# Query weight parts and query tile 1 pulled into the gated part, and a new order at the end of the attention, in a two-layer hybrid encoder step

## What is computed

```
h = rms_norm(x, w_norm1);  proj = h @ w_in          # columns a, gc, gb | q | k, v, u | vg
y_conv = gb * conv3(gc * a)                         # 256 wide
q, k   = partial_rope(q), partial_rope(k)
y_attn = sink_softmax(q @ k.T / 8, band mask) @ v   # 8 heads, 2 kv heads, 512 wide
u  = gelu(u);  vg = layer_norm(gelu(vg), ln_g, ln_b)
y_gmlp = u * (W_s vg + b_s)                         # per chunk of 128 rows, 4 groups, 256 wide
mix = concat(rms_norm(y_conv), rms_norm(y_attn), rms_norm(y_gmlp))   # each with its part of w_group_norm
x = x + mix @ w_out
x = x + relu(rms_norm(x, w_norm2) @ w_ff1)**2 @ w_ff2
```

## Time and profile before

| | us |
|---|---|
| median of 3 runs | 2365.97 |
| lowest, highest | 2364.42, 2366.91 |
| the profiled execution: its own time | 2366.66 |
| the profiled execution: span, first to last instruction | 2364.6 |
| TensorE busy in it | 2303.7 (97%) |
| VectorE, ScalarE, GpSimd busy | 1275.5, 817.8, 125.6 |
| mean granted TensorE clock | 0.991 of full |

### The profile page before, as it was taken

The page is one execution under the profiler, slowest core; times in us unless marked ns, Lnnn a source line. Parts: engine busy times, 40 slices in busy tenths (PEclk is TensorE's granted clock), DMA queues, the critical chain, the costliest instruction groups (busy, mean ns, idle before and its releaser), DMA issues. The chain is left out here.

```text
span 2364.6 us, 32179 instructions
## 1 busy us (share of the span) xinstructions
PE 2303.7 (97%) x12710; PEld 2054.7 (87%) x12710; DVE 1275.5 (54%) x2205; ACT 817.8 (35%) x1697; POOL 125.6 (5%) x223
## 2 busy tenths in 40 slices
PE   7998999999999999999999999999999999999997
PEld 6987878999999988888898877779999999888885
DVE  5226865434344385765752477663334344766766
ACT  4123422444444432122231234234444444222222
POOL 4010100000000000000130100010000000000001
PEclk9999999999999999999999999999999999999999
DMA  6011001346555786656230110114545549766562
GB/s 175 32 33 44 19 29 43 111 174 219 201 185 210 282 318 233 242 194 241 98 70 28 33 45 19 44 37 148 209 176 216 201 170 357 267 233 252 184 232 115
DMA packets 190374, 361.67 MB, mean 153 GB/s; under 512 B 13308, under 2 KB 96800, under 8 KB 190224
## 3 DMA queue, kind: packets, MB, share of 16 engines
q1 hardware_dynamic: 186368, 352.33, 41.1%
q0 software_dynamic: 2704, 3.10, 0.6%
q10 hardware_dynamic: 1152, 4.19, 0.5%
HBM read 228.01 MB, written 131.37 MB: 152 GB/s over the span
## 5 line engine op out<-in xcount | busy, mean ns | idle before, releaser
L1555 PE MATMUL ps<-hT_hi,w_hi 128*128 128x384 f32 x1824 | 614.7, 337 | 2.7 <-DVE x L1208 2.7
L1556 PE MATMUL ps<-hT_lo,w_hi 128*128 128x384 f32 x1824 | 612.9, 336 | 0.0
L1557 PE MATMUL ps<-hT_hi,w_lo 128*128 128x384 f32 x1824 | 612.9, 336 | 0.0
L1556 PE MATMUL ps<-w_lo,ring 128*128 128x512 f32 x896 | 354.7, 396 | 0.0
L1555 PE MATMUL ps<-w_hi,ring 128*128 128x512 f32 x896 | 352.2, 393 | 0.0
L1557 PE MATMUL ps<-w_hi,ring 128*128 128x512 f32 x896 | 352.0, 393 | 0.0
L1555 PEld LDWEIGHTS ps<-hT_hi,w_hi 128*128 128x128 f32 x1824 | 342.9, 188 | 3.2 <-DVE x L1208 3.1
L1556 PEld LDWEIGHTS ps<-hT_lo,w_hi 128*128 128x128 f32 x1824 | 343.0, 188 | 0.0
L1557 PEld LDWEIGHTS ps<-hT_hi,w_lo 128*128 128x128 f32 x1824 | 342.9, 188 | 0.0
L1053 DVE TENSOR_TENSOR w_lo<-w_raw,w_hi 128x512 fp32r<-128x512 f32 (+1 forms) x232 | 143.5, 668 | 345.0 <-ACT w_hi L689 345.0
L1555 PE MATMUL ps<-w_hi,hT_hi 128*128 128x512 f32 (+1 forms) x720 | 278.5, 387 | 5.8 <-ACT vn L892 4.5
(11 more groups left out here) (205 smaller groups left out, 2626.6 us busy)
## 6 DMA issues: line engine op xcount, KB each, us to landing
ff_ops<-row_op SPq DMA_DIRECT2D x224, 512.0 KB, 3.9
ring<-ff_ops SPq DMA_DIRECT2D x56, 2048.0 KB, 8.2
w_raw<-in_w_ff SPq DMA_DIRECT2D x128, 256.0 KB
b<-in_w_ff SPq DMA_DIRECT2D x24, 1024.0 KB, 13.9
w_raw<-in_w_in SPq DMA_DIRECT2D x56, 256.0 KB
w_raw<-in_w_out SPq DMA_DIRECT2D x32, 256.0 KB
ff_last<-last_op SPq DMA_DIRECT2D x32, 256.0 KB, 4.2
w_raw<-in_w_ff SPq DMA_DIRECT2D x8, 1024.0 KB, 10.5
```

What stands on the lines that cost most here:

```text
L1555: pe.matmul(out, sh, mh, start=first, stop=False)
L1556: pe.matmul(out, sh, ml, start=False, stop=False)
L1557: return pe.matmul(out, sl, mh, start=False, stop=last)
```

## The change

**Gated part.** ScalarE splits query units 0 and 1 in step i = 7, before the squares of tile 5; then gelu of tile 8, units 2 and 3, the copy back of tile 5, units 4 to 7, squares and copy back of tile 6, the copy of query tile 0 out of its bank, and then tiles 7 and 8. The squares go to `sq6` instead of `aT`, which shares its place with `qn`. VectorE splits units 0 to 3 before the moments of tile 8, and units 4 to 7 between the normalisations of tiles 7 and 8; the last three tiles' bias and gate steps follow. Normalising takes two instructions instead of three, for all tiles. TensorE makes the second half of query tile 0 ahead of the transposes of tile 6, and the first half of query tile 1 ahead of those of tile 7, if `qn_raw` of tile 0 is there; the attention loop then only has the second half of tile 1.

**End of the attention.** TensorE's `side_rows(0, 0)` stands before `scores(TS)`. VectorE's `group_scale` of tile 5 stands before the softmax of tile 8, `group_scale` of tile 7 directly behind `mixed_rows` of tile 8, and the splits of output units 4 to 7 behind both.

Core of the diff:

```diff
@@ scalar, gated part
-                        if i == TS:
-                            split(range(U_Q, U_Q + 4))
                         act.wait_ge(*(vg_full.at(i) if i < TS else released(U_VG + 7)))
...
+                    if i == TS - 1:
+                        split(range(U_Q, U_Q + 2))
+                    if i >= 2:
+                        gate_square(i - 2)
                     if i >= 3:
...
+                        gated_back(i - 3)
+                gate_rows(TS)
+                split(range(U_Q + 2, U_Q + 4))
+                gated_back(TS - 3)
+                split(range(U_Q + 4, U_Q + 8))
+                gate_square(TS - 2)
+                gated_back(TS - 2)
+                copy_q(0)
+                for t in (TS - 1, TS):
+                    gate_square(t)
+                    gated_back(t)
@@ vector, gated part
-                        link(V.tensor_scalar(row, row, mv[:, t % 2, 0:1], rln[:, t % 2:t % 2 + 1], ALU.subtract,
-                                             ALU.mult))
-                        link(V.tensor_tensor(row, row, lng[:], ALU.mult))
-                        V.tensor_tensor(row, row, lnb[:], ALU.add).then_inc(*vn_ready.tick(t))
...
+                    link(V.scalar_tensor_tensor(row, row, mv[:, t % 2, 0:1], lng[:], ALU.subtract, ALU.mult))
+                    V.scalar_tensor_tensor(row, row, rln[:, t % 2:t % 2 + 1], lnb[:], ALU.mult,
+                                           ALU.add).then_inc(*vn_ready.tick(t))
...
+                split(range(U_Q, U_Q + 4))
+                gate_moments(TS)
+                gate_norm(TS - 1)
+                split(range(U_Q + 4, U_Q + 8))
+                gate_norm(TS)
+                for t in (TS - 2, TS - 1, TS):
+                    gate_mix(t)
@@ tensor, gated part
+                    if i == T:
+                        rows_by_cols(ps[:, 0, :], 0, U_Q, range(KD // 2, KD), sum_of=range(KD)).then_inc(*q_full.tick(0))
+                    if i == T + 1:
+                        pe.wait_ge(*qn_raw.at(0))
+                        rows_by_cols(ps[:, 0, :], 1, U_Q, range(0, KD // 2), sum_of=range(KD))
                     if i >= 3:
                         gated_turn(i - 3)
```

130 lines of the change are left out of this document (62 added, 68 removed).

## The result

The changed kernel takes 2337.11 us in the median of four runs (2335.9 to 2339.18), the kernel before 2366.44 us beside it on the same chip (four runs, 2364.42 to 2367.68). The ratio is 0.9877 with a 95% interval of 0.9862 to 0.9891. The forecast was 2337. The profiled execution has a span of 2337.0 us against 2364.6, so 27.6 us have to be found in the trace.

The account below looks back on a forecast made before the run. TensorE's list was taken to bound the kernel, so only waits and low clock count: 7.5 + 6.9 + 4.0 + 3.7 + 2 x 3.25 + 1.7 = 30.3 us, less 1.3, gives 2337 us; 8 in 10 range 2330 to 2347.

Parts of the forecast that it names:

- What bounds the kernel: Whole kernel: TensorE, busy 2303.7 of 2364.6 us, sets the end; only its waits and low-clock time can be won.
- the six stretches: Stretches of 3.4 or 6.8 us at half clock, 34.0 us in all, each at or right behind a TensorE wait.
- Gated part, 7.5 and 6.9 us: Chunk mix of tile 6 to first scores: 18.5 us instead of 26.0 and 25.4, with a new 1.3 us wait.
- Last scores, 4.0 and 3.7 us: Scores behind side rows: 1.36 us wait filled, scores 2.5 us (between 1.7 and 3.4); gain per layer, ends 3.1 and 4.8.
- Sums, 3.25 us a layer: Before the group sums: waits of 0.85 and 2.40 us gone in each layer, plus 1.7 us of low clock in layer 1.
- The work behind (projection, norm, feed-forward) follows TensorE and keeps its own waits.: Behind the attention: no new waits expected, so no term in the sum.
- the 0.5 us of side row 6: Margin by which the addition of side row 6, now behind four low parts, was to be done before side rows 7.
- 1.3 us for a low stretch that may come back: Taken off the summed gain for one half-clock stretch that may return in one of the layers.
- 1, clock stays low: Waits go but low-clock stretches stay, costing about 12 of the 30 us: 2348 us; chance 0.16.
- 2, weights pace the gated part: Loads of units 4 to 7 land 1.5 us later, costing 3.2 us a layer: 2343 us; in part, 0.14 with the next.
- 3, no effect of the gated moves: VectorE's last gate steps hand over as late as before, about 4 us a layer stay: about 2343; shares 0.14.
- 4, low clock in the attention loop: New gaps bring low stretches to the loop's 18 passes, 1.7 us each: slower, about 2370 us; chance 0.03.

Follow-up runs that it names:

- The old tail: Changed kernel with the end of the attention ordered as before, the gated part staying changed: 2354.85 us, ratio 0.9930 to the kernel before.
- the run without early splits: Changed kernel with all four high parts of query units 0 to 3 in a row ahead of the gelu of tile 8: 2338.01 us, 0.9872.
- three instructions: Changed kernel with the normalisation of the gated rows in three instructions again, not two fused ones: 2341.35 us, 0.9892 of the kernel before.
- after: The changed kernel itself, in its first measurement: 2337.11 us, 0.9877 of the kernel before.
- scores first: Changed kernel with the scores of the samples ahead of side rows 0 again: 2350.89 us, 0.9926 of the kernel before.
- filler: Kernel before with five unused products added in the 1.36 us wait ahead of the scores of the samples: 2364.22 us, 0.9989.
- no half ahead: Changed kernel without the first half of query tile 1 ahead of the last gated transposes: 2345.99 us, 0.9914 of the kernel before.
- gate step with loads as two: Changed kernel with tile 6's gate step between query units 5 and 6 and each slow output weight load as two transfers: 2340.01 us, 0.9878.

## Why the prediction was right

The mechanism was right in the main, and the time too; that it was right to a microsecond is luck. The same kernel, measured again, took 2345.36 us, inside the range of 8 in 10 (2330 to 2347) and outside the 2331 to 2341 that the forecast called itself right for. The span's gain is 27.6 us. The forecast added up 30.3 us and took 1.3 off; the same stretches gave 26.4. By its steps:

- **What bounds the kernel.** TensorE's waits and the low clock behind them: right. The old tail brings back waits and low stretches together, and products in the wait keep the clock up. The reading that the six stretches are the only ones behind the start missed those at the kernel's end (2354.2 us on), which no product meets.
- **Gated part, 7.5 and 6.9 us.** Measured 7.15 and 6.48. The chain came as worked out, the new late wait too (1.15 us, forecast 1.3). The first scores came at 209.34, as worked out (209.4), but the stretch began 0.42 us sooner than in the kernel before (190.49), and the chain did not come sooner with it. The term that was too small is the landing of unit 6, at about 197.0 instead of 196.4:

```profile
197.03 1.27 ACT L689 ACTIVATE w_hi<-w_raw 128x512 fp32r<-128x512 f32 x2 [0.78 <-DMA w_raw<-in_w_in]
...
197.69 1.33 DVE L1065 TENSOR_TENSOR w_lo<-w_raw,w_hi 128x512 fp32r<-128x512 f32 x2 [0.72 <-ACT w_hi L689]
```

  VectorE's last low part ends at 199.0 instead of 198.5, and the transposes of tile 6 follow at 201.25 instead of 200.8. The fused instruction, taken at 0.43 us and measured at 0.485, adds only 0.1 us behind that: the two of tile 7 stand ahead of VectorE's wait for the loads. The reading behind it was half right: a wait that is removed ahead of a late chain is only moved, as the run without early splits shows. The forecast did take the end from VectorE's chain and not from the sum of TensorE's waits, so the number held.
- **Last scores, 4.0 and 3.7 us.** Measured 4.53 and 4.23. The scores at full clock take 2.0 us and not 2.5. The low bound of 1.7 (halved) was the nearer end, and the mean of the ends was too careful. The full gain also needed the 6.8 us at half clock of this one trace of the kernel before; with 3.4 us, as in the other two kernels with the old order, the order is worth 3.0 us.
- **Sums, 3.25 us a layer.** Measured 3.74 and 3.71 from the values to side rows 7, so this and 0.5 us more. In layer 0 it can be followed by the starts: from the transposes ahead of the first waiting sums to the products behind them TensorE takes 1.09 us less, for a wait of 0.85, and around the second 2.65 us less, for one of 2.40. A removed wait was worth about a quarter of a microsecond more than its row says, which is the small price of the last section.
- **"The work behind (projection, norm, feed-forward) follows TensorE and keeps its own waits."** This step was wrong. New waits of 1.90 and 1.01 us stand before the projection, the first with a stretch at half clock. The forecast looked at what the moved splits wait for and at who waits for their neighbours in the list, down to the 0.5 us of side row 6, but not at what their end triggers: the next four loads, two DMA engines wide and 5.35 us each, with an addition queued behind the last. It costs 3.7 us in layer 0. In layer 1 it costs 1.3 us (67.28 against 66.01), and the low stretch of before is won, for 1.5 us: together +0.27.
- **1.3 us for a low stretch that may come back.** It came, not in the gated part but behind the new wait, and covered a quarter of what the missed step cost against the sum: 3.7 us in layer 0 and 1.4 in layer 1, where 0.27 us arrived of the 1.7. The rest was made up by the last scores and the sums, 2.0 us above their terms, and by the 1.2 us that lie in no named stretch. That these cancel is luck. The place was luck as well, the amount was not: in the other traces one comes in the gated part too (20.33, 20.64, 20.67 in the table).
- **Rivals.** 1, clock stays low: no; 2, weights pace the gated part: in a small part, unit 6 landed 0.6 us late and not the 1.5 us it needed; 3, no effect of the gated moves: no; 4, low clock in the attention loop: no, it takes 76.94 us in all kernels.

## What to carry to other kernels

When a split or a copy is moved in an engine's list, follow what its end releases: a load that starts later is late where its result stands in front of something else, many microseconds behind the move. Look in the windows at the DMA share while such a load runs; a transfer that uses 0.13 of the engines can be cut so that it uses more, and its order then no longer matters. Price a wait by trying what the next late thing is: here the second longest wait in the list was worth a quarter of its length, and half a tile of products put into an idle stretch was worth 5 us, nearly twice its own length.

## What was not expected of the hardware

**The price of a wait has two values.** Behind a wait for `x` of 1.0 to 2.0 us, the stretch from the last sums to the norm takes 66.01 us, the wait and either 0.26 to 0.28 us or 1.81 to 1.82 us more: six of the fourteen passes with such waits in seven traces have the larger one, and in those the granted clock shows a stretch at half. At this place length plays a part: the six waits of 1.01 to 1.77 us all have the small price, the three of 1.98 to 2.02 us the large, and of the five between 1.79 and 1.92 us three have the large. But it doesn't decide alone: a wait of 1.91 us has the small price (three instructions, layer 0), one of 1.90 us the large (after, layer 0), with the same lists around. Nor does it carry over to other places: at the last scores 1.36 us has the stretch at half clock in six of six passes, before the sums 2.40 us in five of six. In the same way the gated part of the changed kernel takes 18.9 or 20.7 us in two executions of the same program. What else decides it stays open; for a forecast, such a stretch is worth 1.55 us, with a chance read from waits of the same length at the same place.

**Products of the same shape differ by 1% between executions at a granted clock of 1.00.** One group of the up projection, in the trace of the run with the scores first and in the second trace of the changed kernel:

```profile
L1574 PE MATMUL ps<-hT_hi,w_hi 128*128 128x384 f32 x1824 | 621.0, 340 | 2.7 <-DVE x L1220 2.7
```

```profile
L1574 PE MATMUL ps<-hT_hi,w_hi 128*128 128x384 f32 x1824 | 615.2, 337 | 2.7 <-DVE x L1220 2.7
```

Where it says 340, the feed-forward of both layers is longer: from the norm of layer 0 to the gated part of layer 1 it is 962.9 us instead of 955.6. Where it says 339 (filler, no half ahead, gate step with loads as two) it is one layer's. It comes in steps of 7 to 8 us and with kernels whose lists there are the same, so it belongs to no edit, but it makes the profiled executions of the runs with the scores first and with the filler 15 and 8 us longer than their changed stretches say, and likely raises the medians there too: the ten times with the scores first come in three groups, 2344.0 to 2344.7, 2349.4 to 2352.7 and 2359.6 to 2361.7 us, with the profiled execution, in which both layers are long, in the last. The lowest group is what A had forecast for that run (2344 to 2346). Its cause was not looked for.
